# A recurrent stage's last weight remainder, made on GpSimd instead of on VectorE

## What is computed

```python
def rglru_mixer(h, w_in, conv_w, conv_b, w_a, b_a, w_x, b_x, lam, w_out):
    z = h @ w_in
    gate, xr = jnp.split(z, 2, axis=-1)
    xr = causal_dwconv(xr, conv_w, conv_b)
    ...
    r = sigmoid(xb @ w_a + b_a)          # block by block
    i = sigmoid(xb @ w_x + b_x)
    log_a = -RG_C * r * softplus(-lam)
    a = exp(log_a)
    b = sqrt(-expm1(2.0 * log_a)) * (i * xr)
    ...                                  # hs[t] = a[t] * hs[t-1] + b[t]
    y = gelu(gate) * hs
    return y @ w_out
```

## Time and profile before

| What | us |
|---|---|
| Time, median of 3 runs (1561.02 to 1562.05) | 1561.12 |
| The profiled execution: its own time | 1558.29 |
| The profiled execution: span from its first to its last instruction | 1556.5 |
| TensorE busy | 1536.6 (99% of the span) |
| VectorE busy | 1145.2 (74%) |
| ScalarE busy | 902.8 (58%) |
| GpSimd busy | 158.2 (10%) |
| TensorE's granted clock, mean over the span (1 is 2.4 GHz) | 0.997 |

### The profile page before, as it was taken

One profiled execution on the slowest core, in us unless ns is written; L12 is line 12 of the kernel. 1 busy time (PEld: TensorE's weight loads), 2 busy tenths in 40 slices (PEclk: granted clock), 3 DMA queues, 4 the chain that ended last, 5 costly groups with the idle time before them and its releaser, 6 DMA issues.

```text
span 1556.5 us, 29834 instructions
## 1 busy us (share of the span) xinstructions
PE 1536.6 (99%) x12768; PEld 1490.2 (96%) x12768; DVE 1145.2 (74%) x1390; ACT 902.8 (58%) x1208; POOL 158.2 (10%) x91
## 2 busy tenths in 40 slices
PE   7999999999999999999999999999999999999998
PEld 7999999999999999899899999999889899999998
DVE  6768878888878787678458875678777647877666
ACT  6656644798645565456465744456645655645444
POOL 0301111010112110000030100010000012010110
PEclk9999999999999999999999999999999999999999
DMA  9345554534555545333244555544442334565552
GB/s 312 133 170 202 199 191 166 179 147 163 181 205 183 189 163 190 136 109 109 86 166 163 190 193 185 189 161 164 167 151 90 109 115 160 175 207 193 186 191 79
DMA packets 38558, 258.68 MB, mean 166 GB/s; under 512 B 4784, under 2 KB 5552, under 8 KB 7984
## 3 DMA queue, kind: packets, MB, share of 16 engines
q1 hardware_dynamic: 38016, 255.27, 47.4%
q10 hardware_dynamic: 432, 1.84, 0.3%
HBM read 256.04 MB, written 1.05 MB: 165 GB/s over the span
## 4 chain that ended last, share of the span: by engine, by line
PE 86%; DVE 6%; ACT 5%; issue 2%; POOL 0%; DMA 0%; SPq 0%; ACTq 0%; DVEq 0%
PE bank L1760 26%; PE bank L1762 25%; PE bank L1761 25%; PE bank L2079 3%; PE bank L2027 3%; DVE w_lo L1024 2%; PE bank L2052 2%; ACT w_hi L502 2%; DVE qk L1140 1%; PE bank L1969 1%; PE bank L1996 1%; POOL y_lo L1682 0%; DVE bank L1090 0%; DVE qk L1467 0%; DMA x<-XT 0%
## 5 line engine op out<-in xcount | busy, mean ns | idle before, releaser
L1760 PE MATMUL bank<-h_hi,w_hi 128*128 128x256 f32 x2640 | 750.6, 284 | 11.3 <-DVE h_lo L1039 9.2
L1762 PE MATMUL bank<-h_hi,w_lo 128*128 128x256 f32 x2640 | 741.1, 281 | 0.0
L1761 PE MATMUL bank<-h_lo,w_hi 128*128 128x256 f32 x2640 | 740.9, 281 | 0.0
L1024 DVE TENSOR_TENSOR w_lo<-raw,w_hi 128x2048 fp32r<-128x2048 f32 x237 | 552.2, 2333 | 165.6 <-ACT w_hi L502 164.6
L502 ACT ACTIVATE w_hi<-raw 128x2048 fp32r<-128x2048 f32 x237 | 452.7, 1912 | 235.8 <-PE bank L1762 235.6
L1760 PEld LDWEIGHTS bank<-h_hi,w_hi 128*128 128x128 f32 x2640 | 497.1, 188 | 23.1 <-issue 19.8
L1762 PEld LDWEIGHTS bank<-h_hi,w_lo 128*128 128x128 f32 x2640 | 500.1, 189 | 0.0
L1761 PEld LDWEIGHTS bank<-h_lo,w_hi 128*128 128x128 f32 x2640 | 496.9, 188 | 0.3
L1760 PE MATMUL bank<-y_hi,w_hi 128*128 128x256 f32 x1040 | 294.1, 283 | 3.0 <-DVE y_lo L1497 1.7
L1762 PE MATMUL bank<-y_hi,w_lo 128*128 128x256 f32 x1040 | 291.4, 280 | 0.0
L1761 PE MATMUL bank<-y_lo,w_hi 128*128 128x256 f32 x1040 | 291.1, 280 | 0.0
(11 more groups left out here) (227 smaller groups left out, 1367.8 us busy)
## 6 DMA issues: line engine op xcount, KB each, us to landing
raw<-W SPq DMA_DIRECT2D x237, 1024.0 KB, 4.8
raw<-W SPq DMA_DIRECT2D x4, 512.0 KB, 7.6
wide<-RW ACTq DMA_DIRECT2D x1, 1280.0 KB, 8.7
x<-XT SPq DMA_DIRECT2D x4, 256.0 KB, 6.2
OUT<-x SPq DMA_DIRECT2D x4, 256.0 KB, 2.0
wide<-CON SPq DMA_DIRECT2D x1, 640.0 KB, 9.4
val<-PE_T ACTq DMA_DIRECT2D x2, 256.0 KB, 2.9
vec<-VEC SPq DMA_DIRECT2D x1, 390.0 KB, 6.4
```

Source lines behind the costliest of these rows:

```text
L1024: V.tensor_tensor(w_lo[:, n0 % NW], raw[:, n0 % NRAW], w_hi[:, n0 % NW].bitcast(F32), ALU.subtract)\
L1760: T.matmul(out, w[0], a[0], start=start, stop=False, **kw)
L1761: T.matmul(out, w[0], a[1], start=False, stop=False, **kw)
L1762: return T.matmul(out, w[1], a[0], start=False, stop=stop, **kw)
```

## The change

The split of o4's weights is taken out of VectorE's `gates(4)`. GpSimd makes it, behind its last `y_lo`, in two halves of 128 x 1024: the first when ScalarE's `w_hi` is there (`hi_done`), the second when VectorE has counted the split of o3 (`lo_done`), so that the count keeps its order. The second half counts o4 in `lo_done`. VectorE waits for that count before its next split, that of the next stage's first unit (`pool_split`).

```diff
                     dve.wait_ge(sems["rgin"], k + 1)
-                    if k + 1 == RG_STEPS:
-
-                        after(at("g4"))
                     dve.wait_ge(sems["rth"], k + 1)
...
+                def pool_split(n0):
+
+                    assert state["split"] == n0
+                    dve.wait_ge(sems["lo_done"], n0 + 1)
+                    state["split"] += 1
...
                         last_low()
 
+                        pool_split(at("g4") + 3)
                         after(at("o2"))
...
                         low(pair(y_lo[:, q % 2], 0), pair(qk, 10), pair(y_hi[:, q % 2], 0)).then_inc(sems["ry_ready"], 1)
+
+                    n0 = B[s] + RG_ORDER.index("g4") + 3
+                    pool.wait_ge(sems["hi_done"], n0 + 1)
+                    w = [(w_lo[:, n0 % NW, a], raw[:, n0 % NRAW, a], w_hi[:, n0 % NW, a])
+                         for a in (slice(0, UW // 2), slice(UW // 2, UW))]
+                    low(*w[0])
+
+                    pool.wait_ge(sems["lo_done"], n0)
+                    low(*w[1]).then_inc(sems["lo_done"], 1)
```

## The result

The changed kernel takes 1564.27 us (median of 10 runs, 1562.16 to 1568.01), the kernel before, run beside it, 1560.98 us (10 runs, 1558.36 to 1562.95). The ratio is 1.0023, with a 95% interval of 1.0014 to 1.0032: slower by 3.3 us, where 1565.1 us and 4.0 us more had been forecast.

What follows compares the result with a forecast made beforehand. TensorE, busy 1536.6 of 1556.5 us, was taken as the bound. A later `y_lo` (+2.15 us) and a lower clock (+1.8) sum to +3.95 us, giving 1565.1 us from a 1561.12 median; range 1562.6 to 1566.5.

Steps and rivals of the forecast that it cites:

- The ceiling: TensorE's idle time between o3 and o4 in the last recurrent step limits any gain to 1.67 us, 0.1%.
- the gain that was aimed at: Without the split on VectorE, the square root and `y_lo` in the last step would come 1.30 us earlier.
- The collision: GpSimd's halves and VectorE's gate lines 1476 and 1483 exclude one another, making these about 2.9 and 2.8 us long.
- The open point: No row showed SCALAR_TENSOR_TENSOR (lines 1476, 1483) against GpSimd; taken to collide, +2.15 us, otherwise +0.37.
- Rivals 2 and 3: Gate instructions keep their 0.7 us: half a collision, +0.37 us, chance 0.08; or `y_lo` 1.30 us earlier, chance 0.06.
- `y_lo`: End of the last step's chain, forecast 2.15 us later, at 382.17, because VectorE waits for GpSimd.
- The standstill: TensorE's idle time between o3 and o4, forecast to grow from 1.67 to 3.82 us.
- The clock: TensorE's granted clock falls to 0.50 some 2.1 us into the idle time before o4, costing 1.8 us.
- Rival 1: The collision happens but TensorE's clock holds through o4: +2.15 us, 1563.3 us, chance 0.2.
- What was costed at nothing: SyncE's later load three units behind o4 and VectorE's added wait before the next stage's first split: no cost.
- The sum: Whole kernel: +2.15 us of delay and 1.8 us of clock, +3.95 us, giving 1565.1 us, chance 0.58.

Runs made afterwards that it cites:

- 32 columns: Kernel before, but VectorE splits only 32 of o4's 2048 columns in the last gate step and GpSimd gets nothing; ratio to before 0.9998.
- the memset: Changed kernel, but GpSimd's two halves only write zeros into o4's remainder instead of subtracting; ratio to the kernel before 0.9998.
- quarters: Changed kernel, but GpSimd's split of o4 is cut into four pieces of 512 columns instead of two of 1024; ratio to before 1.0022.
- two pieces on VectorE: Kernel before, but VectorE splits o4 as 1536 columns in the old place and 512 behind line 1483; ratio to before 1.0006.
- the filled kernel: Changed kernel with 26 useless matmuls on TensorE between o3 and o4; ratio to the kernel before 1.0021.

## Why the prediction was right

Step by step:

- **The ceiling and the gain that was aimed at** (1.30 us earlier): right. With 32 columns `y_lo` comes 1.31 us earlier.
- **The collision.** Right, and to the size: 2.89 and 2.78 us were measured for the two gate instructions, 2.9 and 2.8 were expected. The open point was whether SCALAR_TENSOR_TENSOR collides like TENSOR_TENSOR. It does, and so do the scans (2.25 against 1.27 us); the memset, which doesn't read SBUF, holds nobody up. The Trainium skill's rule on two SBUF inputs (SBUF — State Buffer, "Who interferes with whom") agrees with the trace for all three forms and for the memset. Rivals 2 and 3 are out: each needed those instructions to keep their 0.7 us.
- **`y_lo`**: 2.15 us later was forecast; 2.09 is measured (16.81 against 14.72).
- **The standstill**: 3.82 us forecast, 3.49 measured. `y_lo` was met; o3 ended 0.27 us later in the changed kernel (378.55 - 365.18 = 13.37 us after the last block products, 378.40 - 365.30 = 13.10 before), at TensorE's other pace (last section).
- **The clock**: the mechanism was right, the term was mis-sized, 1.8 us against 1.46. The stretch at 1.2 GHz was taken to begin 2.1 us into the standstill and to last 4.9 to 6.7 us, after the program's start, its end and one place in the middle. It began 3.4 us into the standstill, just as o4 started, and lasted about 3.4 us. So all of it held work, and 0.44 x 3.4 = 1.5 us, the price by the prediction's own share. (By the two distances, 0.21 and 0.119 us, the share is 43%, which changes nothing.) The beginning was taken too early and the length too long; the two errors nearly cancelled, and that 1.8 came so near is in part luck. Rival 1, the clock that holds, is out for this kernel in both profiles; with quarters it came true in one of two.
- **What was costed at nothing**: VectorE's next split starts at 381.90, directly behind `y_lo`, so its added wait costs nothing; TensorE has no new wait on a load.
- **The sum**: +3.95 us forecast; the stretch gives +3.55, the medians +3.29 (2.2 to 5.0 by the interval). The 0.2% (3.1 us) below which the prediction calls a difference no change lies inside that interval, so the medians alone leave it open whether the time is slower by more than that.

The profiled executions as a whole differ by more, 1561.9 against 1556.5 us of span. ScalarE's weight copies, the same in number in both kernels, show where the other 1.8 us come from, all of it behind the stretch. Around 650 us the kernel before loses 3.1 us to a fall of the clock that the changed kernel's first profile doesn't have, around 1143 us it is the changed kernel that loses 1.5, and from 1362 us on the kernel before gains 4.0 by TensorE's quicker pace (another 0.5 us go the other way near 1100). The clock rows are the changed kernel around 650 us, the kernel before around 1143, and the changed kernel there:

```profile
648.80:655.50 6.70, 6.70 (x45) 5.74 (x45) 2.90 (x3) 2.97 (x5) 0.00 (x0) 1.00 0.04 13
```

```profile
1143.20:1146.50 3.30, 3.30 (x26) 3.20 (x26) 3.30 (x4) 0.79 (x3) 0.00 (x0) 1.00 0.19 25
```

```profile
1143.20:1146.50 3.30, 3.30 (x14) 3.03 (x13) 3.30 (x5) 0.62 (x3) 0.00 (x0) 0.50 0.22 30
```

In the second profiles, 1561.6 against 1556.3 us, the pace is the same, and the fall near 1143 makes up most of what the stretch doesn't. Whether that fall has to do with the change is open: it is in both profiles of the changed kernel and in neither of the kernel before, but also in the runs with 32 columns and with two pieces on VectorE, which move nothing to GpSimd.

## What to carry to other kernels

Work that is moved from VectorE to GpSimd is not moved out of VectorE's way where both read SBUF and VectorE's next instructions take two inputs from there: each of these waits until the GpSimd instruction ahead of it is done. Find the cover in the trace first (a row in which the two meet, and its excess length), and, where such a move has to be made, cut GpSimd's work into pieces no longer than the chain can bear (four pieces instead of two gave back 0.94 of `y_lo`'s 2.09 us here, and at 1.0022 the kernel was still slower than before), or place it beside VectorE instructions with one SBUF input. Such a one is line 1455, whose other input is in PSUM: GpSimd's `y_lo` of the earlier trace rows began inside it, and both took what they take alone, 0.68 and 1.30 us.

```profile
368.26 0.68 DVE L1455 TENSOR_TENSOR qk<-bank,rinv_t 128x512 f32<-128x512 f32 x1
```

A stall of TensorE that grows can cost more than its own length: here 2.1 us of waiting brought 1.5 us of lower clock behind it.

## What the runs showed of the hardware that was not expected

**Two paces of TensorE at one granted clock.** The same stream of matmuls runs at one of two distances, and stays with it over long stretches. Matmuls between 1400 and 1500 us, all within the same stage, in the first and the second profile of the kernel before:

```profile
1400.00:1500.00 100.00, 100.00 (x867) 100.00 (x867) 66.60 (x65) 50.08 (x46) 9.03 (x6) 1.00 0.56 189
```

```profile
1400.00:1500.00 100.00, 100.00 (x847) 100.00 (x847) 65.24 (x62) 47.07 (x43) 8.89 (x6) 1.00 0.56 189
```

867 against 847 in 100 us, at a granted clock of 1.00: 115 ns from one to the next, against 118. It is the same kernel, so the pace belongs to the execution; in the filled kernel's two profiles it was 847 and 867 there, the other way round. In that stage alone it is worth some 4 us, more than the whole change. What sets it is open.

**A fall of the clock that is not fixed by the standstill's length.** After 1.39 and 1.67 us the clock stayed, after 3.49 us it fell both times, and after 2.57 and 2.58 us it did in one execution and not in the other. It also falls where TensorE has not stood still: the longest standstill between o4 and the last matmul is 0.89 us in the first profile of the kernel before and 0.83 in that of the changed one, yet the clock fell at 649 us in the one and at 1143 in the other. Of the twelve profiles here five fall near 650 us and nine near 1140, for 1.5 or some 3 us each, in kernels with the change and without. With the two paces they make executions differ by several us. What sets them is open.
